# Head loads in column halves, reordered tile preparation and later residual gate pairs in a gated conv/pool encoder step

## What is computed

```
h = rmsnorm(x) * g_pre
xa, ba, ca, za, xb, zb, ga, gb = split(h @ w_in)            # 1024 -> 8 x 1024
ya = ((ba * conv3(ca * xa)) * silu(za)) @ w_a_out
mixed_g = (mean_W(xb_g) - xb_g) @ w_grp[g],  W in 2, 4, 8, 16
yb = (mixed * pool_scale * silu(zb)) @ w_b_out
o = (sigmoid(ga) * ya + sigmoid(gb) * yb) @ w_o
x1 = x + rmsnorm(o) * g_post
out = x1 + (p @ w_ple) * sigmoid(x1 @ w_pgate)
```

## Time and profile before

| | us |
|---|---|
| median of 3 runs | 746.31 |
| all three runs | 748.84, 746.31, 746.25 |
| the profiled execution | 746.43 |
| its span on the slowest core (core 7) | 744.9 |
| TensorE busy on that core | 733.0 (98%) |
| VectorE, GpSimd, ScalarE busy | 456.0, 408.8, 246.7 |

### The profile page before, as it was taken

The page is one execution under the profiler, slowest core; times in us unless marked ns, Lnnn a source line. Parts: engine busy times, 40 slices in busy tenths (PEclk is TensorE's granted clock), DMA queues, the critical chain, the costliest instruction groups (busy, mean ns, idle before and its releaser), DMA issues.

```text
span 744.9 us, 13638 instructions; the slowest of 8 cores (741.9 to 744.9 us)
## 1 busy us (share of the span) xinstructions
PE 733.0 (98%) x4183; PEld 366.9 (49%) x4183; DVE 456.0 (61%) x779; ACT 246.7 (33%) x458; POOL 408.8 (55%) x514
## 2 busy tenths in 40 slices
PE   7999999999999999999999999999999999999997
PEld 4784444444444444454444454555555555554443
DVE  4566656965465555557687667468746555555646
ACT  3434343322222212343434433232322222224542
POOL 5143444557778772454637746545876766603541
PEclk9999999999999999999999999999999999999999
DMA  8959998755467677686644764354335545034674
GB/s 186 227 112 167 182 167 162 130 86 90 64 106 121 102 114 127 101 140 117 151 80 132 122 113 100 45 84 72 52 52 101 74 69 86 8 113 94 161 158 139
DMA packets 67035, 83.93 MB, mean 113 GB/s; under 512 B 35858, under 2 KB 37394, under 8 KB 66964
## 3 DMA queue, kind: packets, MB, share of 16 engines
q0 software_dynamic: 31152, 48.31, 43.9%
q1 hardware_dynamic: 35808, 34.73, 18.9%
q10 hardware_dynamic: 4, 0.00, 0.0%
HBM read 115.25 MB, written 9.26 MB: 167 GB/s over the span
## 4 chain that ended last, share of the span: by engine, by line
PE 92%; DMA 6%; issue 0%; DVE 0%; ACT 0%; POOL 0%; SPq 0%; DVEq 0%; ACTq 0%; POOLq 0%
PE ps L535 59%; PE ps L711 16%; PE ps L798 7%; PE ps L843 4%; DMA slab<-w_in 3%; PE ps L651 2%; DMA x1T<-hb 2%; PE ps L549 1%; DMA xt<-xp 1%; PE ps L837 1%; PE ps L901 1%; DVE xt L817 0%; PE ps L497 0%; ACT hb L819 0%; DVE xt L854 0%
## 5 line engine op out<-in xcount | busy, mean ns | idle before, releaser
L535 PE MATMUL ps<-hT,slab 128*128 128x512 bf16 (+1 forms) x1952 | 349.5, 337 | 1.4 <-DMA slab<-w_in 1.3
L535 PEld LDWEIGHTS ps<-hT,slab 128*128 128x128 bf16 x1952 | 170.9, 98 | 174.3 <-issue 1.6
L420 POOL DMA_DIRECT2D slab<-w_in x128 | 70.5, 554 | 116.4 <-PE ps L535 86.8
L721 DVE TENSOR_TENSOR tmp<-ps,tmp 128x512 f32<-128x512 f32 x84 | 55.9, 687 | 47.9 <-PE ps L711 41.4
L624 DVE SCALAR_TENSOR_TENSOR qT<-tmp,XB 128x512 bf16<-128x512 f32 (+1 forms) x38 | 33.8, 897 | 63.5 <-POOL tmp L620 63.2
L535 PE MATMUL ps<-qT,slab 128*128 128x512 bf16 (+1 forms) x320 | 64.7, 347 | 0.0
L535 PE MATMUL ps<-vT,slab 128*128 128x512 bf16 (+1 forms) x320 | 64.7, 347 | 0.0
L798 PE MATMUL ps<-wo_sb,mT 128*128 128x512 bf16 x272 | 61.8, 379 | 0.0
L620 POOL TENSOR_TENSOR tmp<-tmp 128x524 f32<-128x524 f32 (+5 forms) x60 | 58.7, 995 | 0.8
L620 POOL TENSOR_TENSOR tmp<-XB 128x526 f32<-128x526 f32 (+1 forms) x38 | 42.6, 1127 | 26.1 <-ACT XB L606 25.7
L733 ACT ACTIVATE tmp<-tmp 128x512 f32<-128x512 f32 x48 | 30.1, 630 | 68.8 <-DVE tmp L721 66.9
(11 more groups left out here) (142 smaller groups left out, 1014.4 us busy)
## 6 DMA issues: line engine op xcount, KB each, us to landing
slab<-w_in POOLq DMA_DIRECT2D x128, 256.0 KB, 6.0
xt<-xp SPq DMA_DIRECT2D x30, 512.0 KB, 6.6
yp<-xt SPq DMA_DIRECT2D x14, 512.0 KB, 3.1
slab<-w_a_out POOLq DMA_DIRECT2D x16, 256.0 KB, 4.3
slab<-w_b_out POOLq DMA_DIRECT2D x16, 256.0 KB, 6.1
wo_sb<-w_o POOLq DMA_DIRECT2D x4, 512.0 KB, 6.3
hT<-w_pgate POOLq DMA_DIRECT2D x4, 512.0 KB, 6.2
xt<-xs SPq DMA_DIRECT2D x2, 512.0 KB, 4.2
```

What stands on the lines that cost most here:

```text
L420: OP('pool', lambda e, d: d(e.dma_start(out=v.ap[:], in_=src)), writes=[v], sem=dsem(v, "ld"), dur=0.56, mb=0.52, key=key, nb=nb, lat=lat ...
L535: ins = e.matmul(b.ap[:, 0:N], lhsT=w.ap[:, kk, :], rhs=act[:, kk, k.rel:k.rel + N], start=(kk == 0), stop=(kk == nk - 1))
L721: OP('dve', lambda e, d: d(e.tensor_tensor(out=out.ap[:, 0:512], in0=b.ap[:, :], in1=a.ap[:, 0:512], op=ALU.add)), reads=[a, b], writes=[o ...
```

## The change

It does five things.

1. The x tiles 0 and 1 are each loaded by two DMAs of 512 columns. The first half goes on SP's queue as before, the second on ScalarE's queue, behind the two g_pre loads. The square and the scaling wait for both halves.
2. The planner's latencies change: for the x loads of tiles 1 and 2 (2.0 to 1.0 and 3.6 to 4.9), and for the six slabs of j = 0 (1.0, 2.2, 2.4, 2.3, 2.3, 2.3 to 1.5, 3.2, 3.8, 3.5, 3.3, 3.0).
3. The second half of tile 0's scaled x is written to a buffer of `p_xT` instead of one of `p_h`.
4. The copies of tiles 2 and 3 from PSUM to hT move from VectorE to ScalarE, with a planned duration of 0.6 in place of 0.69.
5. The gate pairs stand 4 units later in the plan (`kg = ks[1] + 28`), and the p @ w_ple products 1.8 units later still relative to `kg` (6.2 in place of 4.4).

`pg_sums` gets an engine argument that no call sets. With its default it issues the same four subtractions as before.

```diff
             kx = key - (30 if by_pe else 22)
             if by_pe and gi >= 4:
                 kx = 17.6 + 1.0 * (gi - 4)
-            OP('sp', lambda e, d: d(e.dma_start(out=x.ap[:], in_=tl.x)), writes=[x], sem=dsem(x, "ld"), dur=0.4, mb=0.52, key=kx, nb=kx, after=after, lat=[0.9, 2.0, 3.6, 4.5, 5.0, 5.0, 5.0, 6.4][gi] if by_pe else 10.0)
+            two = by_pe and gi < 2
+            xh = [res(f"xh{gi}")] if two else []
+            if two:
+                OP('act', lambda e, d: d(e.dma_start(out=x.ap[:, 512:1024], in_=tl.x[:, 512:1024])), writes=xh, sem=fsem(f"ld_xh{gi}"), dur=0.4, mb=0.26, key=-18 + gi)
+            OP('sp', lambda e, d: d(e.dma_start(out=x.ap[:, 0:512], in_=tl.x[:, 0:512]) if two else e.dma_start(out=x.ap[:], in_=tl.x)), writes=[x], sem=dsem(x, "ld"), dur=0.4, mb=0.26 if two else 0.52, key=kx, nb=kx, after=after, lat=[0.9, 1.0, 4.9, 4.5, 5.0, 5.0, 5.0, 6.4][gi] if by_pe else 10.0)
...
-               reads=[x, res("stats")], writes=[h, ss], dur=1.25, key=key)
+               reads=[x, res("stats")] + xh, writes=[h, ss], dur=1.25, key=key)
...
-            hh = [h] + [val(p_h) for _ in parts[1:]]
+            hh = [h] + [val(p_xT) for _ in parts[1:]]
+            flat = lambda v: v.ap[:] if v.pool is p_h else v.ap[:].rearrange("p k c -> p (k c)")
...
-                   reads=[x, rs] + gs, writes=[hv], dur=1.3 * (c1 - c0) / 1024 + 0.05, key=key)
+                   reads=[x, rs] + xh + gs, writes=[hv], dur=1.3 * (c1 - c0) / 1024 + 0.05, key=key)
...
-                    OP('dve' if gi else 'act', lambda e, d, b=b, k0=k0, k1=k1: (d(e.tensor_copy(out=dst[:, k0:k1, :], in_=b.ap[:].bitcast(BF16)[:, k0 * 128:k1 * 128].rearrange("p (k c) -> p k c", c=128))) if gi else
+                    OP('dve' if gi > 3 or gi == 1 else 'act', lambda e, d, b=b, k0=k0, k1=k1: (d(e.tensor_copy(out=dst[:, k0:k1, :], in_=b.ap[:].bitcast(BF16)[:, k0 * 128:k1 * 128].rearrange("p (k c) -> p k c", c=128))) if gi > 3 or gi == 1 else
...
-                ke = kg + 4.4 + 0.9 * n
+                ke = kg + 6.2 + 0.9 * n
...
-        w01 = [{s: load_slab(wblock(w_in, s * 8 + j), -20.0 + i, 2.2 if j == 0 else 8.0 + 1.5 * i, (1.0, 2.2, 2.4, 2.3, 2.3, 2.3)[i] if j == 0 else (3.7, 3.3, 4.3, 5.7, 7.0, 9.5)[i]) for i, s in enumerate(P1SECS)} for j in range(2)]
+        w01 = [{s: load_slab(wblock(w_in, s * 8 + j), -20.0 + i, 2.2 if j == 0 else 8.0 + 1.5 * i, (1.5, 3.2, 3.8, 3.5, 3.3, 3.0)[i] if j == 0 else (3.7, 3.3, 4.3, 5.7, 7.0, 9.5)[i]) for i, s in enumerate(P1SECS)} for j in range(2)]
...
-            phase3_pair(i0.tiles[n:n + 2], ks, ks[1] + 24.0, T1)
+            phase3_pair(i0.tiles[n:n + 2], ks, ks[1] + 28.0, T1)
```

More of the change, by code:

```diff
@@ L486, in phase0 @@
                 gs = [res("g_bc0")] if k1 == 4 else [res("g_bc1")] if k0 == 4 else [res("g_bc0"), res("g_bc1")]
-                OP('dve', lambda e, d, hv=hv, c0=c0, c1=c1: d(e.scalar_tensor_tensor(out=hv.ap[:, c0:c1], in0=x.ap[:, c0:c1], scalar=stat(2, gi), in1=g_bc[:, c0:c1], op0=ALU.mult, op1=ALU.mult)),
-                   reads=[x, rs] + gs, writes=[hv], dur=1.3 * (c1 - c0) / 1024 + 0.05, key=key)
+                OP('dve', lambda e, d, hv=hv, c0=c0, c1=c1: d(e.scalar_tensor_tensor(out=flat(hv)[:, c0:c1], in0=x.ap[:, c0:c1], scalar=stat(2, gi), in1=g_bc[:, c0:c1], op0=ALU.mult, op1=ALU.mult)),
+                   reads=[x, rs] + xh + gs, writes=[hv], dur=1.3 * (c1 - c0) / 1024 + 0.05, key=key)
                 if by_pe:
@@ L496, in f_tr @@
                         for k in range(k0, k1):
-                            ins = e.transpose(out=b.ap[:].bitcast(BF16)[:, k * 128:(k + 1) * 128], in_=hv.ap[:, k * 128:(k + 1) * 128], identity=ident_b[:])
+                            ins = e.transpose(out=b.ap[:].bitcast(BF16)[:, k * 128:(k + 1) * 128], in_=flat(hv)[:, k * 128:(k + 1) * 128], identity=ident_b[:])
                         d(ins)
@@ L500, in phase0 @@
                     first = [res("hT0_0a")] if len(parts) > 1 else []
-                    OP('dve' if gi else 'act', lambda e, d, b=b, k0=k0, k1=k1: (d(e.tensor_copy(out=dst[:, k0:k1, :], in_=b.ap[:].bitcast(BF16)[:, k0 * 128:k1 * 128].rearrange("p (k c) -> p k c", c=128))) if gi else
+                    OP('dve' if gi > 3 or gi == 1 else 'act', lambda e, d, b=b, k0=k0, k1=k1: (d(e.tensor_copy(out=dst[:, k0:k1, :], in_=b.ap[:].bitcast(BF16)[:, k0 * 128:k1 * 128].rearrange("p (k c) -> p k c", c=128))) if gi > 3 or gi == 1 else
                                                                  d(e.copy(out=dst[:, k0:k1, :], in_=b.ap[:].bitcast(BF16)[:, k0 * 128:k1 * 128].rearrange("p (k c) -> p k c", c=128)))),
-                       reads=[b] + (first if n else []), writes=first if len(parts) > 1 and n == 0 else [ht], dur=0.69 if gi else 0.6, key=key)
+                       reads=[b] + (first if n else []), writes=first if len(parts) > 1 and n == 0 else [ht], dur=0.69 if gi > 3 or gi == 1 else 0.6, key=key)
                 else:
-                    OP('sp', lambda e, d, hv=hv: d(e.dma_start_transpose(out=dst, in_=hv.ap[:])), reads=[hv], writes=[ht], sem=dsem(hv, "tr"), dur=1.3, mb=0.7, key=key)
+                    OP('sp', lambda e, d, hv=hv: d(e.dma_start_transpose(out=dst, in_=flat(hv))), reads=[hv], writes=[ht], sem=dsem(hv, "tr"), dur=1.3, mb=0.7, key=key)
         def blkview(ap, k):
@@ L859, in phase3, with pg_sums @@
                 OP('sp', lambda e, d: d(e.dma_start(out=tl.y, in_=x.ap[:])), reads=[x], writes=[res(f"y{gi}")], sem=dsem(x, "st"), dur=0.35, mb=0.52, key=kg + 6, out=True)
-        def pg_sums(homes, key, deps):
+        def pg_sums(homes, key, deps, eng='dve'):
             y = [[wpg_sb[:, 4 * r:4 * r + 4, 512 * b:512 * b + 512] for b in range(2)] for r in range(2)]
@@ L867, in pg_sums @@
             for n, (in0, in1, rd) in enumerate(((y[0][1], y[0][0], []), (y[1][1], ta[0], [tv[0]]), (y[1][1], y[0][1], []), (y[1][0], ta[1], [tv[1]]))):
-                OP('dve', lambda e, d, n=n, in0=in0, in1=in1: d(e.tensor_tensor(out=ta[n], in0=in0, in1=in1, op=ALU.subtract)),
-                   reads=wv + rd, writes=[tv[n]] + homes[n][1], dur=1.43, key=key + 2 * n)
+                for p in ([(0, 4)] if eng == 'dve' else [(2 * i, 2 * i + 2) for i in range(2)]):
+                    OP(eng, lambda e, d, n=n, in0=in0, in1=in1, p=p: d(e.tensor_tensor(out=ta[n][:, p[0]:p[1], :], in0=in0[:, p[0]:p[1], :], in1=in1[:, p[0]:p[1], :], op=ALU.subtract)),
+                       reads=wv + rd, writes=[tv[n]] + homes[n][1], dur=1.43 if eng == 'dve' else 2.3, key=key + 2 * n)
             return ta, tv, [r for _, r in homes]
```

## The result

The changed kernel took 753.41 us (median of 6 runs), the kernel before 746.64 (median of 6). The ratio is 1.0082, with an interval of 1.0067 to 1.0097, so it is slower, by 0.8%: 6.8 us between the two medians, 6.1 by the ratio. One of the changed kernel's runs took 852.62, on a die whose clock was down throughout; it is left out of the ratio. The profiled execution took 753.79.

What follows compares the result with a forecast made beforehand. TensorE, busy 733.0 of 744.9 us on the slowest core, bounds the kernel. From the profiled 746.43, -1.0 (gate pairs) and -0.3 (head) give 745.1; with the median 0.12 lower, 745.0 us, range 742.8 to 748.3.

Steps and rivals of the forecast that it cites:

- Sign: Whole kernel: the same within 0.5% at chance 0.86, faster by more at 0.10, slower by more at 0.04.
- the likeliest case: Whole kernel: the forecast itself, 745.0 us, with its own range 744 to 746.3 and chance 0.36.
- x in halves from two queues: Head, x1's landing from 7.90: bounds 1 us earlier to 2 us later, taken as 0.
- cost nothing there: Head, ScalarE's two extra DMA issues, about 0.37 us each: free before its first square, which waited for x anyway.
- The slower rival: Head, tile 1's square: x1's second half comes late, slower from a landing at 10.1 us; 748.2 us, chance 0.13.
- clock term: Head, for x1 landing at 11 us: a clock rise 2 us later costs 1 us more.
- The rule on spreading DMAs: Head, x loads: by the skill page halves bring nothing; as a rival only the x1T wait goes, 745.3 us, chance 0.17.
- the fast rival: Head: its gain comes through whole and the clock rises sooner, about -2.1 us more, 743.2 us, chance 0.22.
- The pairs: First residual gate pair, 4 us later: x1T wait goes on every core, -1.0 us on core 7, bounds -1.0 and 0.
- Stores and x loads: After the pair, stores 5.8 us later may delay VectorE's x addition near 374; bounds 0 and +4, taken as 0.
- The buffer and the head's order: Head: 0.59 us wait goes, tile 1's chain gains 0.6 to 1.2 us; whole head -0.3, bounds -1.7 and +1.1.
- ScalarE's copies: Head, copies of tiles 2 and 3: 1.05 us per 1024 columns; effect between -0.3 and +0.35, taken as 0.

Runs made afterwards that it cites:

- e13_g_ahead: Kernel before with the g_pre halves moved to the front of SP's queue, x tiles whole but issued 0.8 us later: 750.01 us, ratio 1.0010.
- e3_one_queue: Changed kernel with both column halves of x tiles 0 and 1 on SP's queue, tile by tile: 750.26 us, ratio 1.0045.
- e10_first: Changed kernel with the two second halves of x ahead of the g_pre halves in ScalarE's queue: 750.67 us, ratio 1.0022.

## Why the prediction was wrong

The forecast was 745.0 us, in 742.8 to 748.3, and the kernel took 753.41 against a before that stayed at 746.64. Sign, range and the likeliest case all failed, and by one step: what two DMAs per tile from two queues do to the landing of x.

- **x in halves from two queues: the step that failed.** It bounded tile 1's landing by 1 us earlier to 2 us later and took 0. Measured by the square: 6 to 10 us later (13.77 to 17.02 over the cores, against 6.62 to 7.90). The 2 us came from 128 packets at a third of the packet rate, counted from 5.3 us on. It assumed that three quarters of a megabyte were through by then, as if both queues moved x together from the start. In fact ScalarE's queue had sent 2 packets by SP's 100 from 3 to 4 us on core 6, and by 5.3 us 0.56 MB of x were through there. The text had the second halves leave at 1.8 us and put no price on it. The table above is that price: even whole rows on one queue, issued 0.6 to 0.7 us later, have tile 1 4 to 6 us late (`e13_g_ahead`), and halves on one queue 5 to 6 (`e3_one_queue`).
- **Tile 0 was never bounded at all.** The text says that the two issues on ScalarE "cost nothing there", because it waited for x anyway, and looks at the landing of x1 alone. Tile 0 came 2.4 to 7.2 us later (7.69 to 12.38 against 4.96 to 5.63). The row that should have raised the question was its own: g_pre takes 0.73 us of ScalarE's issue time, so the second half of tile 0 leaves 0.8 us after the first, on another queue.
- **The slower rival had the mechanism and the place, and the wrong size.** It named the square of tile 1, x1's second half coming late, and a point of decision at 10.1 us. At 13.8 to 17.0 us this was passed on every core. Its price of 748.2 was reckoned for a landing at 11, and its chance of 0.13 rested on "the part of it that moves before they do is not slowed by them" (they are the slabs), which holds only for what is issued first. Its clock term of 1 us was counted beside the delay, though a late rise is part of a late start (above).
- **The rule on spreading DMAs.** The Trainium skill ("DMA: Bandwidth & Descriptors", "Rules for kernel authors") says that spreading DMAs over the issuing engines does not help bandwidth. The prediction took that to mean that the halves are "worth nothing". As to bandwidth it holds here: from 4 to 5.2 us 0.20 MB moved in the changed kernel (core 6) and 0.38 in the one with whole tiles (core 5), and from 4 to 6 us on core 7 it was 0.56 and 0.58, so the second queue gained nothing. As a forecast of time it failed, since not being served faster is not the same as costing nothing.
- **A figure in the fast rival.** Its spacings of 0.107 and 0.056 us do not follow from the 9 and 14 matmuls of the earlier trace rows. They do follow from the groups of eight on core 7, which took 1.06 us at 16.26 with 311 ns for one, and 0.61 at 20.58 with 219.
- **The pairs: right, near -1.0.** Alone they gave -0.27% (-2.0 us, interval -1.2 to -2.8). The interval ends just above the forecast's size; cores 0 and 3 end 0.5 and 0.4 us before core 7 with waits of 1.5 and 2.1, so all three had to gain, as they did. What makes it 2.0 rather than 1.0 the runs do not show. The size of the move was off: 2.2 us instead of 4 on core 7, so waits of 0.4 to 0.6 stayed on three cores. What counts is the matmuls in front of the pair, and the prediction read the plan's units as TensorE's time.
- **Stores and x loads.** The feared wait of VectorE for x came in, some 40 us later than named: 2.65 to 4.54 us on every core of the changed kernel (3.45 at 415.51 on core 7) and 4.42 to 5.51 with the pairs alone, where the kernel before has none from 355 to 430 us. No wait of TensorE follows from it from 400 to 440 us on any core, so 0 was right.
- **The buffer and the head's order: right in size.** The 0.59 us wait went, tile 1's projections came at 13.2 to 14.0 with whole tiles against 14.60, and the slab took most of it. With the buffer alone they did not come earlier on most cores, so the start at 13.2 to 14.0 needs the rest of the head's changes too. The rest of the head measured -0.08% (-0.6 us, interval -1.4 to +0.2), where -0.3 was forecast.
- **ScalarE's copies: right.** A copy of 1024 columns took 1.01 us, estimated at 1.05.

Without the halves the sum nearly stands: whole tiles took 1.9 us less than the kernel before (0.7 to 3.1), where 1.3 less was forecast. The two parts measured alone, 2.0 and 0.6, come to 2.6, so they do not add up exactly, and some of the nearness is luck. Everything that was costed from a row was right to about 1 us; what was costed from no row was off by 6 to 10.

What stays open: why the queue that is issued 0.7 to 0.8 us later gets hardly a packet until after 4 us, though two queues issued together share from the start (`e10_first`) and later three do. The runs show that it is so in both directions, not by what. Open too is why so few bytes move in all from 4 to 6 us in `e3_one_queue`, and so how much of the halves' cost is the size of the packets and how much the later issue.

## What to carry to other kernels

The first loads of a kernel race the bulk loads, and here less than 1 us at issue decided the race: it became 4 to 6 us at the landing. So issue what the first compute needs first, and count every DMA ahead of its last part. Splitting a load adds issues (about 0.4 us each here) and puts the last part back, and a consumer that waits for both parts is as late as the later one. A second queue is no harm as long as its part is issued as early as the first (`e10_first`), but then something else is later. And where no row shows how a resource will behave, the range has to go as far as the whole transfer coming last, for every tile that is touched.

## What the runs showed of the hardware

- Two hardware queues issued 0.7 to 0.8 us apart did not share at first: 100 packets to 2 (3 to 4 us, changed kernel, core 6), and with the roles swapped 93 to 2 in the same stretch (core 0), then 46 to 1. Issued together they did share, 103 to 99. Later the three active queues had 129, 127 and 125 in 4 us.
- Turns go by packets, and a packet was a row of the load: 186 packets for 0.35 MB in column halves, 96 for 0.36 MB in whole rows. Alone the queue moved the same bytes from 3 to 4 us; beside the slabs it moved 0.45 MB against 0.60 in 4 us.
- Tile 1's load, issued 0.6 to 0.7 us later and otherwise the same, was used 3.7 to 5.8 us later; from 4 to 6 us the slabs' queue had 31 to 108 packets beside it against 1 to 26.
- With halves on one queue all queues together moved 0.18 to 0.26 MB from 4 to 6 us, against 0.41 to 0.58 with whole tiles. The cause is not shown.
- A PSUM to SBUF copy of 1024 bf16 columns took 1.01 us on ScalarE and 0.69 on VectorE.
